# A convolving feed-forward rebuilt on products of 512 columns, with its first taps moved to ScalarE

## The chip, the cores and the metric

The kernel runs on one core of one Trainium2 chip. The metric is the device time of one execution in microseconds (us), the median of several runs. The core has TensorE (PE in the profile, with its weight loads shown as PEld), VectorE (DVE), ScalarE (ACT), GpSimd (POOL) and the DMA queues that SyncE (SP) feeds. TensorE's clock has two levels, 1.2 and 2.4 GHz; the profile shows the granted one as 0.50 and 1.00.

## The reference, cut to what matters

The program is a chain of two small transformer blocks on 256 positions with a width of 1024. The part that is touched is the feed-forward of the first block. Unlike the four later ones, it convolves gate and up over positions with three taps before the activation.

```python
def causal_dwconv(x, w):          # out[t] = sum_i w[i] x[t-2+i], per channel
    ...
def conv_ffn(hn, w_up, conv_w, conv_b, w_down):   # hn (1, 256, 1024), w_up (1024, 5632)
    u = causal_dwconv(hn @ w_up, conv_w) + conv_b
    gate, val = jnp.split(u, 2, axis=-1)          # 2816 channels each
    return (jax.nn.silu(gate) * val) @ w_down     # (2816, 1024)

h = h + conv_ffn(rms_norm(h, norm_ffn[l]), ffn_up[l], ffn_conv_w[l], ffn_conv_b[l], ffn_down[l])
```

## The kernel before

**Numbers in two parts.** Everything is stored with channels on partitions and positions along the free axis. A float32 product is made from operands split into a high and a low part: high weights by high operand, high weights by low operand, low weights by high operand. The weights come from memory as 260 slabs of 128 x 2048 (16 blocks of 128 x 128, 1 MB each) through a ring of three slots. For each slab SyncE issues one transfer into `ring_raw`, ScalarE copies it rounded into `ring_hi` (the "hi split"), and VectorE subtracts to get `ring_lo` (the "lo split"). ScalarE may write a slot when TensorE has multiplied the slab three before (`multiplied` counts slabs); SyncE may refill the raw slot when the lo split of the slab three before is done.

**The order of work** is written out by hand for each engine and no engine leaves its order: an instruction that waits holds up all that stands behind it on that engine.

**The feed-forward** goes over 11 pairs of 256 gate channels and 256 up channels. Its slabs are gate 0, up 0, then for each pair p from 1 to 10 the three slabs gate p, up p, down p-1, and at last down 10. Below, G, U and D with a number are these slabs and the products made from them. A loop of 5 turns carries two pairs each on every engine, so there are 10 passes for the pairs 1 to 10; pair 0 stands ahead of the loop and D10 behind it.

**The convolving feed-forward before** (`conv_feed_forward`, three functions, for PE at L518, ACT at L1339, DVE at L1946) makes G and U with `output_slab`: for each of the 16 blocks three products of 256 columns, into one bank of PSUM for a slab. Four banks (0 and 2 for gates, 1 and 7 for ups) alternate, banks 3 to 6 hold the sum of the down projection. VectorE takes the whole work between: it multiplies the sums by the row norm `inv` on the way out of PSUM (L1837), makes the first tap with the bias (L1965) and the two later taps (L1970, L1976), two instructions for each tap, multiplies with the activated gate, and subtracts for `hidden_lo` (L1834). ScalarE gives Silu and the copy `hidden_hi`.

**The plain feed-forward** (`feed_forward`, ffn_0 to ffn_3) makes G and U with `wide_slab`: high and low part of the operand lie side by side in X2, so a block needs one product of 512 columns (high weights) and one of 256 (low weights). Each slab then fills two banks, and each bank holds two halves that must be added. ScalarE copies one half out (`gate_copy`, `up_copy`), VectorE adds the other to it (`add_half`) and the banks are free when this is done (`halves_added`). Gate has banks 0 and 1, up has 2 and 3, down 4 to 7.

The wide product is this:

```python
out, w = bank(first + m), slice((m * KT + k) * P, (m * KT + k + 1) * P)
mm(out, ring_hi[:, slot, w], X2[:, k].rearrange("p s t -> p (s t)"), k == 0, False)
return mm(out[:, 0:T], ring_lo[:, slot, w], XH[:, k, :], False, k == KT - 1)
```

Of the kernel before, what the change touches and what calls it, by code (L numbers as in the profile page):

```python
# [108 lines left out]
def program(nc, ins, out_t):  # L109
    ctx = ExitStack()  # L110
    with ctx:
# [270 lines left out]
        def _(pe):  # L382
# [135 lines left out]
            def conv_feed_forward(name):  # L518

                g0, n = START[name], ffns[0]  # L520
                split, gate_scaled, up_taken = sem("hidden_lo"), sem("gate_scaled"), sem("up_taken")

                def down(at, odd, i, pairs):
                    slot, _, g = place(at, i, 6)
                    pe.wait_ge(lo_split, g + 1)
                    pe.wait_ge(split, pairs)
                    for k in range(2):
                        for m in range(KT):
                            last = block_product(bank(3 + m // 2)[:, m % 2 * T:(m % 2 + 1) * T], slot, k * KT + m,
                                                 HH[:, odd, k, :], HL[:, odd, k, :], False, False)  # L530
                    last.then_inc(multiplied, 1)

                output_slab(g0, 0, bank(0), fresh=EVERY)
                output_slab(g0 + 1, 0, bank(1), between=norm_sum)
                for b in range(3, 7):
                    for m in range(2):
                        mm(bank(b)[:, m * T:(m + 1) * T], zeros[:, 0:P], zeros[:], True, False)
# [12 lines left out]

                slot, _, g = place(g0 + 32)
                pe.wait_ge(lo_split, g + 1)
                pe.wait_ge(split, (n + 1) * FP)
                for m in range(KT):
                    for k in range(2):
                        last = block_product(bank(3 + m // 2)[:, m % 2 * T:(m % 2 + 1) * T], slot, k * KT + m,
                                             HH[:, 0, k, :], HL[:, 0, k, :], False, k == 1)
                    if m % 2 and m < KT - 1:
                        last.then_inc(sem("down_bank"), 1)
                last.then_inc(multiplied, 1)  # L560
                ffns[0] += 1

            def feed_forward(name):
# [710 lines left out]
        def _(act):  # L1274
# [546 lines left out]
        def _(dve):  # L1821
# [124 lines left out]
            def conv_feed_forward(name):  # L1946
# [3 lines left out]
                def gate(at, i, pair, b, split=None):  # L1950
# [4 lines left out]
                    if split is not None:  # L1955
                        split_slab(split, i, 6)
# [911 lines left out]
```

## Time and profile before

| | |
|---|---|
| median of 3 runs | 1770.28 us (1767.76 to 1773.57) |
| the profiled execution | 1767.87 us, its span 1765.9 us |
| PE busy | 1710.1 us, 97% of the span |
| DVE busy | 1235.5 us, 70% |
| ACT busy | 876.7 us, 50% |
| mean granted clock | 0.987 |
| the convolving feed-forward | from about 465 to 662 us |

A line of the timeline gives the start, the length, engine, line, operation and tiles; "x2" is two like instructions merged, whose length goes from the start of the first to the end of the second. "[0.39 <-ACT ring_hi L1280]" says that the engine stood idle for 0.39 us before the instruction, until ACT's instruction that writes `ring_hi` ended. Consecutive instructions of one engine overlap a little, so the distance from start to start is what a place in the order costs. L388, L1280, L1834 and L1837 are lines of helpers (one product, one activation, tensor_tensor, multiplication); the tiles say which use it is. `silu_out`, `hidden`, `conv_x` and `conv_acc` all lie in the tile "arena".

### The profile page before, as it was taken

What the parts mean: (1) busy time and instruction counts of PE and PEld (TensorE: products, weight loads), DVE (VectorE), ACT (ScalarE), POOL (GpSimd) and SP (SyncE); (2) the same over time, 40 slices, a digit from 0 to 9 for tenths busy, and PEclk for the clock granted to TensorE, in tenths of its full rate; (3) what the DMA queues carried; (4) which work ended last, traced back from release to release, by engine and by line L of the source; (5) the groups of instructions that cost most, each with busy time, mean ns of one, the idle gap of its engine ahead of it and who ended that gap; (6) DMA issues with size and microseconds to landing.
All of it is one profiled execution on the core that took longest, in us unless ns stands there. A gap on an engine that the chain in (4) does not pass through costs nothing.

```text
span 1765.9 us, 32905 instructions
## 1 busy us (share of the span) xinstructions
PE 1710.1 (97%) x13828; PEld 1599.1 (91%) x13828; DVE 1235.5 (70%) x1299; ACT 876.7 (50%) x924; POOL 37.7 (2%) x40
## 2 busy tenths in 40 slices
PE   7999998999999999999999999999999999999997
PEld 7988898998999998999999999997999987999997
DVE  5767657954788878666895766677666776666666
ACT  4376434533534345444674644466444652554455
POOL 0000000100000000000030000000000000000000
PEclk9999999999999999999999999999999998999999
DMA  7524444452344544554543455452555440354551
GB/s 275 189 96 144 151 145 174 164 194 97 144 181 152 214 154 157 189 190 166 188 150 110 176 210 180 180 187 103 190 197 183 167 165 24 121 196 168 192 187 48
DMA packets 42664, 286.94 MB, mean 162 GB/s; under 512 B 4720, under 2 KB 6896, under 8 KB 9168
## 3 DMA queue, kind: packets, MB, share of 16 engines
q1 hardware_dynamic: 38528, 273.70, 42.7%
q0 software_dynamic: 2816, 10.69, 1.7%
q8 instruction: 72, 1.18, 0.3%
q10 hardware_dynamic: 1232, 1.25, 0.2%
q14 instruction: 16, 0.13, 0.0%
HBM read 281.42 MB, written 4.19 MB: 162 GB/s over the span
## 4 chain that ended last, share of the span: by engine, by line
PE 81%; DVE 11%; ACT 5%; issue 3%; DMA 1%; POOL 0%; DVEq 0%; ACTq 0%
PE PS L388 80%; DVE arena L1837 3%; DVE ring_lo L1834 3%; ACT arena L1280 2%; ACT ring_hi L1280 2%; DVE arena L1834 1%; ACT L1280 1%; DVE operand L1897 1%; DVE inv L1891 0%; DVE residual L1834 0%; DMA ring_raw<-in_w_stream 0%; DMA arena<-in_ple_t 0%; DVE arena L1970 0%; DVE arena L1965 0%; DVE inv L2598 0%
## 5 line engine op out<-in xcount | busy, mean ns | idle before, releaser
L388 PE MATMUL PS<-operand,ring_hi 128*128 128x256 f32 (+1 forms) x4776 | 1126.4, 321 | 23.0 <-DVE operand L1897 14.2
L388 PEld LDWEIGHTS PS<-operand,ring_hi 128*128 128x128 f32 x4776 | 798.6, 193 | 94.4 <-DVE ring_lo L1834 13.4
L388 PE MATMUL PS<-operand,ring_lo 128*128 128x256 f32 x3092 | 876.2, 283 | 2.2 <-issue 2.2
L1834 DVE TENSOR_TENSOR ring_lo<-ring_raw,ring_hi 128x2048 fp32r<-128x2048 f32 x260 | 600.7, 2314 | 192.5 <-ACT ring_hi L1280 192.2
L1280 ACT ACTIVATE ring_hi<-ring_raw 128x2048 fp32r<-128x2048 f32 x260 | 494.6, 1907 | 206.4 <-PE PS L388 201.4
L388 PEld LDWEIGHTS PS<-operand,ring_lo 128*128 128x128 f32 x3092 | 593.8, 192 | 2.6 <-issue 2.5
L388 PE MATMUL PS<-hidden_hi,ring_hi 128*128 128x256 f32 x880 | 249.0, 283 | 1.3 <-DVE hidden_lo L1834 1.3
L388 PE MATMUL PS<-hidden_lo,ring_hi 128*128 128x256 f32 x880 | 249.0, 283 | 0.0
L388 PE MATMUL PS<-hidden_hi,ring_lo 128*128 128x256 f32 x880 | 248.9, 283 | 0.0
L1280 ACT ACTIVATE arena<-PS 128x512 f32<-128x512 f32 (+4 forms) x121 | 79.5, 666 | 302.0 <-PE PS L388 292.5
L388 PEld LDWEIGHTS PS<-hidden_hi,ring_hi 128*128 128x128 f32 x880 | 168.6, 192 | 3.5 <-issue 1.5
L388 PEld LDWEIGHTS PS<-hidden_hi,ring_lo 128*128 128x128 f32 x880 | 168.7, 192 | 0.0
L388 PEld LDWEIGHTS PS<-hidden_lo,ring_hi 128*128 128x128 f32 x880 | 168.6, 192 | 0.0
L1834 DVE TENSOR_TENSOR arena<-arena,PS 128x512 f32<-128x512 f32 (+4 forms) x120 | 81.0, 685 | 110.4 <-ACT arena L1280 108.6
L1280 ACT ACTIVATE arena<-arena 128x512 f32<-128x512 f32 (+5 forms) x117 | 83.2, 722 | 103.7 <-DVE arena L1976 56.8
L388 PE MATMUL PS<-arena 64*64 64x64 f32 (+7 forms) x2264 | 125.9, 249 | 8.8 <-DVE arena L1837 4.1
L388 PEld LDWEIGHTS PS<-arena 64*64 64x64 f32 (+4 forms) x2264 | 109.7, 151 | 24.0 <-issue 5.4
L1280 ACT ACTIVATE hidden_hi<-arena 128x512 fp32r<-128x512 f32 x55 | 34.8, 632 | 111.7 <-DVE arena L1837 111.7
L1837 DVE TENSOR_TENSOR arena<-PS,inv 128x512 f32<-128x512 f32 x74 | 50.5, 687 | 49.8 <-PE PS L388 49.4
L1837 DVE TENSOR_TENSOR arena<-arena 128x512 f32<-128x512 f32 (+3 forms) x96 | 72.8, 768 | 15.2 <-ACT arena L1280 9.1
L1837 DVE TENSOR_TENSOR arena<-arena,inv 128x512 f32<-128x512 f32 x96 | 66.1, 688 | 4.3 <-ACT arena L1280 2.8
L1280 ACT ACT_TABLE_LOAD x49 | 62.9, 1283 | 4.4 <-issue 3.5
(148 smaller groups left out, 942.6 us busy)
## 6 DMA issues: line engine op xcount, KB each, us to landing
ring_raw<-in_w_stream SPq DMA_DIRECT2D x260, 1024.0 KB, 4.8
spilled_gates<-arena POOLq DMA_DIRECT2D x12, 256.0 KB, 2.6
arena<-spilled_gates POOLq DMA_DIRECT2D x2, 1536.0 KB, 9.3
tables<-in_tables POOLq DMA_DIRECT2D x1, 1344.0 KB, 10.7
residual<-in_x_t ACTq DMA_DIRECT2D x4, 256.0 KB, 6.0
arena<-in_mem_t POOLq DMA_DIRECT2D x1, 1024.0 KB, 14.5
out_t<-residual SPq DMA_DIRECT2D x4, 256.0 KB, 2.1
arena<-in_spatial_t POOLq DMA_DIRECT2D x1, 512.0 KB, 4.2
```

The source lines that it names most:

```text
L388: return nc.tensor.matmul(out, lhs, rhs, start=start, stop=stop, skip_group_check=True)
L1280: return nc.scalar.activation(out, in_, func, **kw)
L1834: return v.tensor_tensor(out, a, b, op)
L1837: return v.tensor_tensor(out, a, b, ALU.mult)
L1897: v.scalar_tensor_tensor(out=XL[:, x0 + k, :], in0=src[:, k, :], scalar=col(gain[0], gain[1] + k), in1=XH[:, x0 + k, :].bitcast(F32), op0= ...
```

## The change

The convolving feed-forward gets the plain one's products. On TensorE its own function goes and `feed_forward("ffn_c")` stands in its place, with `wide_slab` and banks 0 and 1 for gate, 2 and 3 for up, 4 to 7 for down. ScalarE copies one half out of each pair of banks and also makes the first tap with the bias (`first_taps`, Identity with scale and bias from `params`). VectorE adds the other half, multiplies by `inv` in SBUF (`scale`) and makes the two later taps. The order on both engines is written anew. The sum for the norm behind the stage moves from bank 7 to bank 3. The counts of `halves_added` and `half_copied` in the plain feed-forwards shift, since ffn_c now counts too.

```diff
@@ TensorE @@
-            def conv_feed_forward(name):
...
-                with pe.Fori(0, FP // 2) as i:
-                    pe.wait_ge(gate_scaled, i * 2 + (n * FP + 1))
-                    output_slab(g0 + 2, 0, bank(2), i, 6)
-                    pe.wait_ge(sem("norm_root"), norms[0])
-                    pe.wait_ge(up_taken, i * 2 + (n * FP + 1))
-                    output_slab(g0 + 3, 0, bank(7), i, 6)
-                    down(g0 + 4, 0, i, i * 2 + (n * FP + 1))
-                    pe.wait_ge(gate_scaled, i * 2 + (n * FP + 2))
-                    output_slab(g0 + 5, 0, bank(0), i, 6)
-                    pe.wait_ge(up_taken, i * 2 + (n * FP + 2))
-                    output_slab(g0 + 6, 0, bank(1), i, 6)
-                    down(g0 + 7, 1, i, i * 2 + (n * FP + 2))
-
...
-                        at, halves = g0 + 5 - 3 * odd, i * 4 + (2 * (n - 1) * FP + 3 - 2 * odd)
+                        at, halves = g0 + 5 - 3 * odd, i * 4 + (2 * n * FP + 3 - 2 * odd)
...
-            conv_feed_forward("ffn_c")
+            feed_forward("ffn_c")
...
-                last = chunk_sums(7, 2 * c, c == 0, c == 3)
+                last = chunk_sums(3, 2 * c, c == 0, c == 3)
@@ ScalarE @@
 
-                def gate(pair, i=0, split=None):
-
-                    if split is not None:
-                        split_slab(split, i, 6)
+                def copy(at, i, half, x, first, free):
+
+                    act.wait_ge(multiplied, place(at, i, 6)[2] + 1)
+                    act.wait_ge(*free)
+                    run(x, sides(first)[:, 1]).then_inc(sem("half_copied"), 1)
+
+                def gate_copy(at, i, pair):
+                    copy(at, i, 0, conv_x[0], 0, (sem("conv_done"), pair))
+
+                def up_copy(at, i, pair):
+                    copy(at, i, 1, conv_x[1], 2, (up_taken, pair + 1))
+
+                def first_taps(acc, x, tile_, scaled, free):
+
+                    act.wait_ge(*scaled)
+                    act.wait_ge(*free)
+                    for m in range(2):
+                        run(acc[:, m, :], x[:, m, :], ACT.Identity,
+                            scale=prm[:, bass.ds(tile_ + (m + COL["ffn_conv_w"] + 2 * 4 * FP), 1)],
+                            bias=prm[:, bass.ds(tile_ + (m + COL["ffn_conv_b"]), 1)]).then_inc(sem("first_tap"), 1)
+
+                def gate_taps(pair, free=True):
+                    first_taps(conv_acc, conv_x[0], pair * 2, (sem("gate_scaled"), pair + 2),
+                               (sem("gate_active"), pair) if free else (sem("gate_scaled"), 1))
+
+                def up_taps(pair):
+                    first_taps(conv_acc2, conv_x[1], pair * 2 + 2 * FP, (sem("conv_up_scaled"), pair + 1),
+                               (up_taken, pair + 1))
+
+                def gate(pair):
+
...
                 split_slab(g0 + 2)
+                act.wait_ge(multiplied, g0 + 1)
+                run(conv_x[0], sides(0)[:, 1]).then_inc(sem("half_copied"), 1)
                 split_slab(g0 + 3)
                 norm_root()
+                up_copy(g0 + 1, 0, 0)
+                gate_taps(0, False)
+                up_taps(0)
                 gate(0)
                 up(0, 0)
                 with act.Fori(0, FP // 2) as i:
-                    split_slab(g0 + 4, i, 6)
-                    gate(i * 2 + 1, i, g0 + 5)
-                    up(i * 2 + 1, 1, i * 6 + (g0 + 2))
-                    split_slab(g0 + 6, i, 6)
-                    split_slab(g0 + 7, i, 6)
-                    gate(i * 2 + 2, i, g0 + 8)
-                    up(i * 2 + 2, 0, i * 6 + (g0 + 5))
-                    split_slab(g0 + 9, i, 6)
+                    for odd in (1, 0):
+                        pair = i * 2 + (2 - odd)
+                        split_slab(g0 + 7 - 3 * odd, i, 6)
+                        gate_copy(g0 + 5 - 3 * odd, i, pair)
+                        gate_taps(pair)
+                        split_slab(g0 + 8 - 3 * odd, i, 6)
+                        up_copy(g0 + 6 - 3 * odd, i, pair)
+                        gate(pair)
+                        up_taps(pair)
+                        split_slab(g0 + 9 - 3 * odd, i, 6)
+                        up(pair, odd, i * 6 + (g0 + 5 - 3 * odd))
...
-            norm_root()
+            norm_root(b=3)
@@ VectorE @@
-                def gate(at, i, pair, b, split=None):
-
-                    dve.wait_ge(multiplied, place(at, i, 6)[2] + 1)
-                    dve.wait_ge(up_taken, pair + 1)
-                    mul(conv_x[0], tiles_of(b, 2), over(inv[:, 0:T], 2)).then_inc(gate_scaled, 1)
-                    if split is not None:
-                        split_slab(split, i, 6)
-                    dve.wait_ge(gate_scaled, pair + 2)
-                    taps(conv_acc, conv_x[0], pair * 2, pair * 11, sem("conv_done"))
...
-                def taps(acc, x, tile_, before, done):
-
-                    for m in range(2):
-                        w2 = prm[:, bass.ds(tile_ + (m + COL["ffn_conv_w"] + 2 * 4 * FP), 1)]
-                        b = prm[:, bass.ds(tile_ + (m + COL["ffn_conv_b"]), 1)]
-                        v.tensor_scalar(acc[:, m, :], x[:, m, :], w2, b, ALU.mult, ALU.add)\
-                         .then_inc(sem("conv_tap"), 1)
-                    dve.wait_ge(sem("conv_tap"), before + 2)
-                    for m in range(2):
...
+                def add_half(x, first, pair, up):
+
+                    dve.wait_ge(sem("half_copied"), pair * 2 + (1 + up))
+                    tt_(x, x, sides(first)[:, 0], ALU.add).then_inc(sem("halves_added"), 1)
+
+                def scale(x, pair, up, done):
+
+                    dve.wait_ge(sem("halves_added"), pair * 2 + (1 + up))
+                    mul(x, x, over(inv[:, 0:T], 2)).then_inc(done, 1)
+
+                def later_taps(acc, x, tile_, first, before, done):
+
+                    dve.wait_ge(sem("first_tap"), first)
+                    for back in (1, 2):
+                        for m in range(2):
+                            w = prm[:, bass.ds(tile_ + (m + COL["ffn_conv_w"] + (2 - back) * 4 * FP), 1)]
+                            v.scalar_tensor_tensor(out=acc[:, m, back:T], in0=x[:, m, 0:T - back], scalar=w,
+                                                   in1=acc[:, m, back:T], op0=ALU.mult, op1=ALU.add)\
+                             .then_inc(done if (back, m) == (2, 1) else sem("conv_tap"), 1)
+                        if back == 1:
+                            dve.wait_ge(sem("conv_tap"), before + 2)
+
+                def gate_taps(pair):
+                    later_taps(conv_acc, conv_x[0], pair * 2, pair * 4 + 2, pair * 7, sem("conv_done"))
+
+                def up_taps(pair):
+                    later_taps(conv_acc2, conv_x[1], pair * 2 + 2 * FP, pair * 4 + 4, pair * 7 + 3, sem("conv_tap"))
+
+                def up(pair, odd):
+
+                    dve.wait_ge(sem("conv_tap"), pair * 7 + 7)
+                    dve.wait_ge(gate_active, pair + 1)
                     dve.wait_ge(sem("hidden_lo"), pair)
-                    mul(conv_x[1], tiles_of(b, 2), over(inv[:, 0:T], 2)).then_inc(sem("conv_up_scaled"), 1)
-                    dve.wait_ge(sem("conv_up_scaled"), pair + 1)
-                    taps(conv_acc2, conv_x[1], pair * 2 + 2 * FP, pair * 11 + 5, sem("conv_tap"))
-                    dve.wait_ge(sem("conv_tap"), pair * 11 + 11)
-                    dve.wait_ge(gate_active, pair + 1)
                     mul(hidden, silu_out, flat(conv_acc2)).then_inc(up_taken, 1)
                     dve.wait_ge(sem("hidden_hi"), pair + 1)
                     tt_(flat(HL[:, odd]), hidden, flat(HH[:, odd]).bitcast(F32), ALU.subtract)\
                         .then_inc(sem("hidden_lo"), 1)
 
...
                 with dve.Fori(0, FP // 2) as i:
-                    split_slab(g0 + 4, i, 6)
-                    gate(g0 + 2, i, i * 2 + 1, 2, g0 + 5)
-                    up(g0 + 3, i, i * 2 + 1, 1, 7)
-                    split_slab(g0 + 6, i, 6)
-                    split_slab(g0 + 7, i, 6)
-                    gate(g0 + 5, i, i * 2 + 2, 0, g0 + 8)
-                    up(g0 + 6, i, i * 2 + 2, 0, 1)
-                    split_slab(g0 + 9, i, 6)
+                    for odd in (1, 0):
+                        pair = i * 2 + (2 - odd)
+                        split_slab(g0 + 7 - 3 * odd, i, 6)
+                        add_half(conv_x[0], 0, pair, 0)
+                        scale(conv_x[0], pair, 0, gate_scaled)
+                        split_slab(g0 + 8 - 3 * odd, i, 6)
+                        gate_taps(pair)
+                        add_half(conv_x[1], 2, pair, 1)
+                        scale(conv_x[1], pair, 1, sem("conv_up_scaled"))
+                        split_slab(g0 + 9 - 3 * odd, i, 6)
+                        up_taps(pair)
+                        up(pair, odd)
...
-            down("ffn_c", None, scale=1.0, first=3)
+            down("ffn_c", None, scale=1.0)
```

## Rows read from the trace of the kernel before

**Rows 1.** The page: the chain that ended last, shares of the span by engine.

```profile
PE 81%; DVE 11%; ACT 5%; issue 3%; DMA 1%; POOL 0%; DVEq 0%; ACTq 0%
```

**Rows 2.** Windows: stretch, length, busy time (instructions) of each engine, clock, DMA; one pass each.

```profile
566.00:583.27 17.27, 17.27 (x147) 17.27 (x146) 14.26 (x20) 6.79 (x5) 0.00 (x0) 1.00 0.46 182
...
770.60:787.74 17.14, 17.14 (x115) 15.64 (x114) 10.97 (x10) 7.87 (x7) 0.00 (x0) 1.00 0.51 184
```

**Rows 3.** Timeline of VectorE: one pass of the convolving feed-forward.

```profile
570.57 4.50 DVE L1834 TENSOR_TENSOR ring_lo<-ring_raw,ring_hi 128x2048 fp32r<-128x2048 f32 x2 [1.12 <-ACT ring_hi L1280]
...
576.04 2.29 DVE L1834 TENSOR_TENSOR ring_lo<-ring_raw,ring_hi 128x2048 fp32r<-128x2048 f32 x1 [0.38 <-ACT ring_hi L1280]
578.25 0.73 DVE L1965 TENSOR_SCALAR arena<-arena,params 128x256 f32<-128x256 f32 x2
579.13 0.88 DVE L1970 SCALAR_TENSOR_TENSOR arena<-arena,params 128x255 f32<-128x255 f32 x2 [0.15 <-DVE arena L1965]
580.16 0.88 DVE L1976 SCALAR_TENSOR_TENSOR arena<-arena,params 128x254 f32<-128x254 f32 x2
580.95 0.68 DVE L1837 TENSOR_TENSOR arena<-PS,inv 128x512 f32<-128x512 f32 x1
...
583.74 0.88 DVE L1976 SCALAR_TENSOR_TENSOR arena<-arena,params 128x254 f32<-128x254 f32 x2
584.64 0.69 DVE L1837 TENSOR_TENSOR arena<-arena 128x512 f32<-128x512 f32 x1
586.04 0.69 DVE L1834 TENSOR_TENSOR hidden_lo<-arena,hidden_hi 128x512 fp32r<-128x512 f32 x1 [0.70 <-ACT hidden_hi L1280]
587.84 4.49 DVE L1834 TENSOR_TENSOR ring_lo<-ring_raw,ring_hi 128x2048 fp32r<-128x2048 f32 x2 [1.11 <-ACT ring_hi L1280]
```

**Rows 4.** Timeline of ScalarE in the same pass.

```profile
574.09 1.92 ACT L1280 ACTIVATE ring_hi<-ring_raw 128x2048 fp32r<-128x2048 f32 x1 [1.75 <-PE PS L388]
...
585.37 0.63 ACT L1280 ACTIVATE hidden_hi<-arena 128x512 fp32r<-128x512 f32 x1 [3.67 <-DVE arena L1837]
585.91 3.70 ACT L1280 ACTIVATE ring_hi<-ring_raw 128x2048 fp32r<-128x2048 f32 x2
```

**Rows 5.** Timeline of VectorE in the plain feed-forward that follows (ffn_0).

```profile
691.49 0.68 DVE L1834 TENSOR_TENSOR arena<-arena,PS 128x512 f32<-128x512 f32 x1
692.20 0.69 DVE L1837 TENSOR_TENSOR arena<-arena,inv 128x512 f32<-128x512 f32 x1
692.81 2.28 DVE L1834 TENSOR_TENSOR ring_lo<-ring_raw,ring_hi 128x2048 fp32r<-128x2048 f32 x1
```

**Rows 6.** Timeline of ScalarE behind the stage: two scaled copies, then a square.

```profile
668.68 0.91 ACT L1280 ACTIVATE operand<-residual,params 128x256 fp32r<-128x256 f32 x2 [2.74 <-DVE residual L2432]
669.49 0.61 ACT L1280 ACTIVATE arena<-residual 128x512 f32<-128x512 f32 x1
```

**Rows 7.** Timeline of VectorE ahead of the loop of the convolving feed-forward.

```profile
474.72 1.75 DVE L1891 RECIPROCAL inv<-root 128x256 f32<-128x256 f32 x1
...
483.03 0.69 DVE L1837 TENSOR_TENSOR arena<-arena 128x512 f32<-128x512 f32 x1
...
486.22 2.29 DVE L1834 TENSOR_TENSOR ring_lo<-ring_raw,ring_hi 128x2048 fp32r<-128x2048 f32 x1 [1.11 <-ACT ring_hi L1280]
```

**Rows 8.** Timeline of TensorE: first product of D10.

```profile
656.00 0.35 PE L388 MATMUL PS<-hidden_hi,ring_hi 128*128 128x256 f32 x1 [1.30 <-DVE hidden_lo L1834]
```

**Rows 9.** Windows: TensorE at the start of the program, and in a pause and after it.

```profile
11.10:16.60 5.50, 5.49 (x26) 5.50 (x27) 4.10 (x8) 4.49 (x7) 0.00 (x0) 1.00 1.00 424
16.60:22.00 5.40, 5.40 (x46) 5.40 (x46) 4.86 (x4) 2.79 (x2) 0.00 (x0) 1.00 1.02 424
501.00:503.20 2.20, 0.05 (x2) 0.02 (x1) 2.20 (x2) 2.20 (x2) 0.00 (x0) 1.00 0.00 0
...
504.80:508.20 3.40, 3.40 (x18) 3.40 (x17) 3.40 (x4) 0.00 (x0) 0.00 (x0) 0.50 0.95 386
```

**Rows 10.** The page: costliest groups, busy time and mean, idle time before; table loads.

```profile
L1280 ACT ACT_TABLE_LOAD x49 | 62.9, 1283 | 4.4 <-issue 3.5
```

More of the change, by code:

```diff
@@ L516, in _ @@
             ffns = [0]
-            def conv_feed_forward(name):
[L520 to L535, printed above, removed]
-                    for m in range(2):
-                        mm(bank(b)[:, m * T:(m + 1) * T], zeros[:, 0:P], zeros[:], True, False)
-                with pe.Fori(0, FP // 2) as i:
-                    pe.wait_ge(gate_scaled, i * 2 + (n * FP + 1))
-                    output_slab(g0 + 2, 0, bank(2), i, 6)
-                    pe.wait_ge(sem("norm_root"), norms[0])
-                    pe.wait_ge(up_taken, i * 2 + (n * FP + 1))
-                    output_slab(g0 + 3, 0, bank(7), i, 6)
-                    down(g0 + 4, 0, i, i * 2 + (n * FP + 1))
-                    pe.wait_ge(gate_scaled, i * 2 + (n * FP + 2))
-                    output_slab(g0 + 5, 0, bank(0), i, 6)
-                    pe.wait_ge(up_taken, i * 2 + (n * FP + 2))
-                    output_slab(g0 + 6, 0, bank(1), i, 6)
-                    down(g0 + 7, 1, i, i * 2 + (n * FP + 2))
[L551 to L561, printed above, removed]
@@ L1960, in taps @@
-                def taps(acc, x, tile_, before, done):
-                    for m in range(2):
-                        w2 = prm[:, bass.ds(tile_ + (m + COL["ffn_conv_w"] + 2 * 4 * FP), 1)]
-                        b = prm[:, bass.ds(tile_ + (m + COL["ffn_conv_b"]), 1)]
-                        v.tensor_scalar(acc[:, m, :], x[:, m, :], w2, b, ALU.mult, ALU.add)\
-                         .then_inc(sem("conv_tap"), 1)
-                    dve.wait_ge(sem("conv_tap"), before + 2)
-                    for m in range(2):
-                        w1 = prm[:, bass.ds(tile_ + (m + COL["ffn_conv_w"] + 4 * FP), 1)]
-                        v.scalar_tensor_tensor(out=acc[:, m, 1:T], in0=x[:, m, 0:T - 1], scalar=w1,
-                                               in1=acc[:, m, 1:T], op0=ALU.mult, op1=ALU.add)\
-                         .then_inc(sem("conv_tap"), 1)
-                    dve.wait_ge(sem("conv_tap"), before + 4)
-                    for m in range(2):
-                        w0 = prm[:, bass.ds(tile_ + (m + COL["ffn_conv_w"]), 1)]
-                        v.scalar_tensor_tensor(out=acc[:, m, 2:T], in0=x[:, m, 0:T - 2], scalar=w0,
-                                               in1=acc[:, m, 2:T], op0=ALU.mult, op1=ALU.add)\
-                         .then_inc(done if m == 1 else sem("conv_tap"), 1)
@@ L1994, in conv_feed_forward @@
                 split_slab(g0 + 2)
+                add_half(conv_x[0], 0, 0, 0)
                 split_slab(g0 + 3)
                 norm_factor()
-                gate(g0, 0, 0, 0)
-                up(g0 + 1, 0, 0, 0, 1)
-                with dve.Fori(0, FP // 2) as i:
-                    split_slab(g0 + 4, i, 6)
-                    gate(g0 + 2, i, i * 2 + 1, 2, g0 + 5)
-                    up(g0 + 3, i, i * 2 + 1, 1, 7)
-                    split_slab(g0 + 6, i, 6)
-                    split_slab(g0 + 7, i, 6)
-                    gate(g0 + 5, i, i * 2 + 2, 0, g0 + 8)
-                    up(g0 + 6, i, i * 2 + 2, 0, 1)
-                    split_slab(g0 + 9, i, 6)
+                add_half(conv_x[1], 2, 0, 1)
+                scale(conv_x[0], 0, 0, gate_scaled)
+                scale(conv_x[1], 0, 1, sem("conv_up_scaled"))
+                gate_taps(0)
+                up_taps(0)
+                dve.wait_ge(sem("conv_tap"), 7)
+                dve.wait_ge(gate_active, 1)
+                mul(hidden, silu_out, flat(conv_acc2)).then_inc(up_taken, 1)
+                dve.wait_ge(sem("hidden_hi"), 1)
+                tt_(flat(HL[:, 0]), hidden, flat(HH[:, 0]).bitcast(F32), ALU.subtract).then_inc(sem("hidden_lo"), 1)
+                with dve.Fori(0, FP // 2) as i:
+                    for odd in (1, 0):
[10 more added lines that the diff above has]
+                        up(pair, odd)
                 ffns[0] += 1
@@ L2015, in add_half @@
                 def add_half(out, first, pair, up):
-                    dve.wait_ge(sem("half_copied"), pair * 2 + (2 * (n - 1) * FP + 1 + up))
+                    dve.wait_ge(sem("half_copied"), pair * 2 + (2 * n * FP + 1 + up))
                     tt_(out, out, sides(first)[:, 0], ALU.add).then_inc(sem("halves_added"), 1)
                 def half_added(pair, up):
-                    dve.wait_ge(sem("halves_added"), pair * 2 + (2 * (n - 1) * FP + 1 + up))
+                    dve.wait_ge(sem("halves_added"), pair * 2 + (2 * n * FP + 1 + up))
                 def gate_scale(pair):
```

2 lines of the change are left out of this document (removed).

## The prediction

> **What bounds the kernel now.** I read the chain that ended last first: 81% of it is TensorE, VectorE has 11% [rows 1]. So on the whole a shorter piece of TensorE work counts. I then read one pass of the stage (one pair, three slabs) by windows. TensorE is busy through all of its 17.27 us, VectorE for 14.26, ScalarE for 6.79 [rows 2]. Busy shares don't say how much room VectorE has, since it waits inside its order; that is read from its timeline. It runs from 570.57 to 587.84, again 17.27, with two lasting waits for ScalarE: 1.11 before the lo split of D, and 0.38 before the one at 576.04 [rows 3]. The second comes from a hi split that ScalarE began late, as TensorE had not finished a slab [rows 4]: this is TensorE's pace showing through. Without it VectorE's order would take 17.27 - 0.38 = 16.89. The reader is to see two orders of nearly one length, TensorE's 17.27 and VectorE's 16.89: a few tenths more on VectorE and it becomes the bound.
>
> **TensorE after.** The plain feed-forward has the new products already, and its pass takes 17.14, with 115 products for 147 (a few records are missing, 144 are made) [rows 2]. Hence 0.13 less for a pair; over 11 pairs 1.4 us. That is all that the wide products can give: the columns stay the same, 768 for a block.
>
> **VectorE's order after, step by step.** I take distances from start to start in one pass, since these are what a place in the order costs; t = 0 is the start of the lo split of D(p-1).
>
> 1. Lo split of D: 578.25 - 576.04 = 2.21 [rows 3]. The add begins at 2.21.
> 2. Add of the gate halves: 692.20 - 691.49 = 0.71 [rows 5]. ScalarE's copy of one half, some 0.6 as the square of the same size (0.61 [rows 6]), lies under the lo split, once G(p) is made.
> 3. Scale of gate at 2.92. Here the new wait begins. ScalarE's order is gate copy, first taps of gate, hi split of G(p+1); VectorE's next instruction is the lo split of that same slab. The first taps wait for the scale, the hi split stands behind them, the lo split waits for the hi split. From an instruction of VectorE to ScalarE's on its result is 585.37 - 584.64 = 0.73 [rows 3, 4]; so the taps start at 3.65. No row of before shows Identity with scale and bias. The nearest are two scaled copies of like size: 0.91 busy for both, 0.81 from start to start of the next [rows 6]. In a loop with coefficients addressed by a register, two taps on VectorE cost 1.03 where they are busy 0.88 [rows 3]. So 0.81 from below and 1.04 from above; I take 0.90. From the start of the hi split to that of the lo split: 576.04 - 574.09 = 1.95 [rows 3, 4]. Step 3 costs 0.73 + 0.90 + 1.95 = 3.58, and the lo split begins at 6.50. Without the wait its distance would be 692.81 - 692.20 = 0.61 [rows 5]: the order loses 2.97.
> 4. Lo split of G(p+1): 2.21, to 8.71.
> 5. Later taps of gate: 580.16 - 579.13 = 1.03 and 580.95 - 580.16 = 0.79, together 1.82 [rows 3], to 10.53. Silu follows under the next steps.
> 6. Add of the up halves 0.71, to 11.24. The up copy lies under step 4.
> 7. Scale of up, and the same knot again: ScalarE has the up taps ahead of the hi split of U(p+1), for which VectorE waits. 3.58 once more, to 14.82.
> 8. Lo split of U(p+1): 2.21, to 17.03.
> 9. Later taps of up: 1.03 + 0.90 (584.64 - 583.74) = 1.93 [rows 3], to 18.96.
> 10. The product `hidden`, ScalarE's `hidden_hi`, `hidden_lo`, ScalarE's hi split of D(p), the lo split of D(p): as before, 587.84 - 584.64 = 3.20 [rows 3].
>
> Sum: 2.21 + 0.71 + 3.58 + 2.21 + 1.82 + 0.71 + 3.58 + 2.21 + 1.93 + 3.20 = **22.16 us** for a pass, against 17.27. VectorE's busy time hardly moves: two pairs of first taps go (2 x 0.73), two adds come (2 x 0.69). What it gains is two waits of 2.97, because ScalarE's short taps now stand between VectorE's scale and the split that VectorE needs next. ScalarE itself would be busy about 6.79 + 2 x 0.61 + 2 x 0.91 = 9.8 of 22.16, and TensorE 17.14: no engine would be full, the order is the bound.
>
> **Does TensorE or a transfer hold this chain?** G(p) can start when its lo split is done, at 6.50 + 2.29 = 8.79 of the pass before; (17.14 - 17.27/3)/2 = 5.7 later it is made, at 14.5, and is copied only after 22. U(p) waits for its lo split, 14.82 + 2.29 = 17.1, and ends at 22.8, 0.6 into the pass; its copy comes after 6.5. D(p-1) waits until 2.29 and ends at 8.05, ahead of G(p+1). So TensorE stands 0.7, 2.6 and 1.7 us in each pass, 5.0 in all, and VectorE never waits for it. The banks come free with the adds, before their products are due. The raw slots are refilled as soon as a lo split ends; each refill has more time than now, so the transfers stay hidden, and SyncE has nothing else in its queue.
>
> **Ahead of the loop.** The add of gate 0 goes between two lo splits. ScalarE's copy stands ahead of the hi split of U1, which puts the norm's reciprocal at about 475.2, now 474.72 [rows 7]. Then add, two scales, the taps of gate (0.73 + 0.90 behind their scale) and 1.8 each for the later taps of gate and up bring `hidden` to 482.9, now 483.03: the first taps run beside VectorE here, as no split stands behind them. I take the start of the loop at 486.2, as now [rows 7].
>
> **Behind the loop.** The tenth pass starts at 486.2 + 9 x 22.16 = 685.6. Its `hidden_lo` starts 18.96 + 1.40 (586.04 - 584.64) in and ends 0.69 later, at 706.7. D10 starts then, now at 656.00 [rows 8]: 50.7 later. D9 was done at 8.05 of that pass, 693.7, so TensorE stands 13 us. The nearest row is the start of the program, after 11.1 us without work: 26 products in the first 5.50 us and 46 in the 5.40 behind them [rows 9], though the clock column shows 1.00 there. The low level (1.2 GHz for 2.4) costs D10 then 5.5 x (1 - 26/46) = 2.4. Bounds: 0 (D10 itself began after a pause of 1.30 at full speed, [rows 8]) and 2.4. I take 2.4, as the pauses are alike. The work behind, with bank 3 for 7 and `first` as 4, is the same: 0.
>
> **Sum.** 50.7 + 2.4 = 53.1 more. The profiled execution had 1767.87, so 1821.0; the median of the runs stands 2.4 above that, so **1823 us**, 3.0% slower.
>
> **A page on Identity.** The Trainium skill, "ScalarE: Activation LUTs", section "Table sets: the hidden batching unit", says that identity and copy lie in every table set. No row of before shows Identity. By the page no table is loaded for the taps, and the sum stays; the rival with table loads below is what it denies.
>
> **The rivals.**
> - *TensorE stays the bound.* Then a pass takes 17.14, the stage gains 1.4, and if the pause of 2.2 at 501 with the slow stretch behind it (18 products in 3.4 us for 28, 1.2 us [rows 9]) and the 1.30 before D10 vanish too, 1.4 + 2.2 + 1.2 + 1.3 = 6.1. Time: 1764 to 1769. For it: ffn_0 does run at TensorE's pace with these products. Against: there only the copy stands ahead of the hi split on ScalarE, nothing that waits for the scale. It decides where VectorE's order falls below 17.14: it is 16.2 with both waits gone (22.16 - 2 x 2.97), so the two together would have to cost under 0.9, and one hi split alone is 1.95. Chance 0.05, of which 0.02 is over 0.3% faster.
> - *Only one of the two waits is paid*, the other being covered by something that I misread in the order. 22.16 - 2.97 = 19.19 for a pass, 29.7 us less: about 1793. Against: both places have the same three instructions. Chance 0.03.
> - *Table loads.* Silu and Identity by turns, each with a load of 1.28 us [rows 10]. The one ahead of Silu lies in idle time; the one ahead of the up taps would begin when Silu ends, at 11.2, and put the taps at 12.5 for 11.97, 0.5 a pass: 1828. Chance 0.05.
> - *The low clock lasts.* A pause of 2.2 us was followed by a stretch at 0.50 [rows 9], and each pass would have a pause of 2.6. One such stretch costs TensorE 1.2 us, two 2.4, and it has 5.0 to spare: no cost. If the low clock holds for whole passes, TensorE needs 17.14 x 46/26 = 30.3 and becomes the bound: 8.2 x 10 = 82 more, 1905. Against: the stretch was short and TensorE then ran on at 1.00. Chance 0.03. The Trainium skill, "TensorE: Matmul & The Clock Gate", section "HAM oscillation — how this bites in real kernels", tells of a kernel whose wait recurs with each tile and whose clock falls in every tile; by that rule one fall in each pass, which the spare time takes in.
>
> **How the numbers follow.** My forecast has 0.84. Its own range: 0.81 to 1.04 for a pair of first taps moves a pass by -0.18 to +0.28, ten passes by -2 to +3; D10's clock 0 to 2.4; a semaphore's 0.1 at some of the six handovers, up to +3; the run's place in its spread, 3 either way. Together 1815 to 1830. With the table loads and some room for sizes that I read wrongly the range is **1812 to 1833**. Outside it lie the first, second and fourth rival. A measurement of this kernel tells about 0.3% (5.3 us) from no change: faster 0.02, same 0.03, slower 0.95.
>
> **What would show it.** Right: VectorE's timeline with waits of about 2.9 before two of its three lo splits in each pass, released by ScalarE's `ring_hi`; passes of 22.2; TensorE pausing about 2.6 for `ring_lo` before U; about 13 us of pause before D10, and the stage's end some 53 us later. Each wide slab 5.7. 49 table loads as now [rows 10]. Wrong: passes near 17.14, or TensorE's products at a pace of 0.2 us throughout the stage; a hi split that starts before the first taps would break the knot at its root.

## The result, and the profile after

| | before | changed |
|---|---|---|
| median | 1770.03 us (4 runs, 1767.76 to 1773.57) | 1828.09 us (4 runs, 1826.41 to 1828.65) |
| ratio | | 1.033, 95% interval 1.0318 to 1.0343: slower |
| profiled execution, its span | 1767.87, 1765.9 us | 1828.55, 1826.6 us |
| mean granted clock | 0.987 | 0.978 |

Every run behind the numbers of this document is a fast one but the fourth of experiment 4, which took 4044.83 us for no reason that its record shows and is left out.

The chain that ended last, by engine, on the page of the changed kernel. Its columns are those of [rows 1].

```profile
PE 72%; DVE 13%; ACT 7%; issue 6%; DMA 1%; DVEq 0%; ACTq 0%; POOL 0%
```

TensorE has lost nine points against [rows 1]; VectorE and ScalarE have gained two each and "issue" three. One pass by windows, with the columns of [rows 2]:

```profile
601.03:623.84 22.81, 19.31 (x115) 16.87 (x113) 14.18 (x18) 9.82 (x12) 0.00 (x0) 0.93 0.40 138
```

The pass lasts 22.81 us for 17.27 [rows 2] and no engine is full in it: TensorE 19.31 (some of it at the low clock), VectorE 14.18, ScalarE 9.82. The reader is to see a longer pass with less work on VectorE. What fills it is seen in VectorE's timeline of that pass, the answer to [rows 3]:

```profile
601.03 2.29 DVE L1824 TENSOR_TENSOR ring_lo<-ring_raw,ring_hi 128x2048 fp32r<-128x2048 f32 x1 [1.11 <-ACT ring_hi L1235]
603.24 0.68 DVE L1824 TENSOR_TENSOR arena<-arena,PS 128x512 f32<-128x512 f32 x1
603.96 0.69 DVE L1827 TENSOR_TENSOR arena<-arena,inv 128x512 f32<-128x512 f32 x1
607.82 2.29 DVE L1824 TENSOR_TENSOR ring_lo<-ring_raw,ring_hi 128x2048 fp32r<-128x2048 f32 x1 [3.17 <-ACT ring_hi L1235]
610.03 1.89 DVE L1956 SCALAR_TENSOR_TENSOR arena<-arena,params 128x255 f32<-128x255 f32 x4
611.84 0.68 DVE L1824 TENSOR_TENSOR arena<-arena,PS 128x512 f32<-128x512 f32 x1
612.55 0.69 DVE L1827 TENSOR_TENSOR arena<-arena,inv 128x512 f32<-128x512 f32 x1
616.35 2.29 DVE L1824 TENSOR_TENSOR ring_lo<-ring_raw,ring_hi 128x2048 fp32r<-128x2048 f32 x1 [3.11 <-ACT ring_hi L1235]
618.56 1.90 DVE L1956 SCALAR_TENSOR_TENSOR arena<-arena,params 128x255 f32<-128x255 f32 x4
620.65 0.69 DVE L1827 TENSOR_TENSOR arena<-arena 128x512 f32<-128x512 f32 x1 [0.19 <-DVE arena L1956]
...
623.84 2.29 DVE L1824 TENSOR_TENSOR ring_lo<-ring_raw,ring_hi 128x2048 fp32r<-128x2048 f32 x1 [1.11 <-ACT ring_hi L1235]
```

Each scale (L1827 with `inv`) is followed by a lo split that waits over 3 us for ScalarE's `ring_hi`. ScalarE's timeline says what it did meanwhile:

```profile
604.89 1.10 ACT L1235 ACTIVATE arena<-arena,params 128x256 f32<-128x256 f32 x2 [3.41 <-DVE arena L1827]
605.89 1.89 ACT L1235 ACTIVATE ring_hi<-ring_raw 128x2048 fp32r<-128x2048 f32 x1
...
613.42 1.09 ACT L1235 ACTIVATE arena<-arena,params 128x256 f32<-128x256 f32 x2 [0.83 <-DVE arena L1827]
614.42 1.90 ACT L1235 ACTIVATE ring_hi<-ring_raw 128x2048 fp32r<-128x2048 f32 x1
```

At 604.89 it had stood for 3.41 us until VectorE's scale was done; then it made the taps, and only then the hi split that VectorE stood for. The waits from 475 to 715 us, nearly the whole stage (engine, tile, line, waited for: total, times, longest):

```profile
DVE ring_lo L1824 <- ACT ring_hi L1235: 75.0, 31, 3.2
...
PE PS L388 <- DVE ring_lo L1824: 35.5, 24, 2.6
...
PE PS L388 <- DVE hidden_lo L1824: 13.4, 1, 13.4
```

TensorE's 13.4 us is the pause before D10. The stage's last add starts at 722.20, 60.2 us later than in the profile of before (662.01).

### The profile page after: what moved, and what is told of

It is laid out like the page before. It is cut to its first block, busy times and chain, and to the rows that moved or that the text cites. A ratio compares the mean times of both kernels' runs of the same rounds, so it can differ in the third digit from the quotient of the medians.

```text
span 1826.6 us, 32297 instructions
## 1 busy us (share of the span) xinstructions
PE 1724.8 (94%) x13476; PEld 1589.9 (87%) x13476; DVE 1234.2 (68%) x1277; ACT 910.5 (50%) x990; POOL 37.6 (2%) x40
## 4 chain that ended last, share of the span: by engine, by line
PE 72%; DVE 13%; ACT 7%; issue 6%; DMA 1%; DVEq 0%; ACTq 0%; POOL 0%
PE PS L388 71%; ACT ring_hi L1235 4%; DVE arena L1827 4%; DVE ring_lo L1824 2%; ACT arena L1235 2%; DVE arena L1956 2%; DVE arena L1824 2%; DVE operand L1887 1%; ACT L1235 0%; DVE inv L1881 0%; DMA ring_raw<-in_w_stream 0%; DVE residual L1824 0%; DMA arena<-in_ple_t 0%; DVE inv L2595 0%; DVEq L1956 0%
## 5 line engine op out<-in xcount | busy, mean ns | idle before, releaser
L388 PEld LDWEIGHTS PS<-operand,ring_hi 128*128 128x128 f32 x4424 | 758.0, 193 | 143.7 <-DVE ring_lo L1824 46.0
L388 PE MATMUL PS<-hidden_hi,ring_hi 128*128 128x256 f32 x880 | 251.3, 286 | 19.4 <-DVE hidden_lo L1824 13.4
L1235 ACT ACTIVATE arena<-PS 128x512 f32<-128x512 f32 (+4 forms) x143 | 92.2, 652 | 306.5 <-PE PS L388 297.1
L1824 DVE TENSOR_TENSOR arena<-arena,PS 128x512 f32<-128x512 f32 (+2 forms) x142 | 96.0, 685 | 112.9 <-ACT arena L1235 109.5
L1827 DVE TENSOR_TENSOR arena<-arena,inv 128x512 f32<-128x512 f32 x118 | 81.2, 689 | 4.9 <-ACT arena L1235 2.8
L1827 DVE TENSOR_TENSOR arena<-arena 128x512 f32<-128x512 f32 (+3 forms) x96 | 72.8, 768 | 16.7 <-ACT arena L1235 9.1
L1235 ACT ACTIVATE arena<-arena,params 128x256 f32<-128x256 f32 x84 | 42.0, 549 | 59.6 <-DVE arena L1827 59.6
L1827 DVE TENSOR_TENSOR arena<-PS,inv 128x512 f32<-128x512 f32 x52 | 35.5, 688 | 50.4 <-PE PS L388 50.1
```

Source lines behind the costliest of these rows:

```text
L388: return nc.tensor.matmul(out, lhs, rhs, start=start, stop=stop, skip_group_check=True)
L1235: return nc.scalar.activation(out, in_, func, **kw)
L1824: return v.tensor_tensor(out, a, b, op)
L1827: return v.tensor_tensor(out, a, b, ALU.mult)
```

## The experiments

Each comparison with before is made on the same chip in alternation. The median of before was 1769.6 us in the first group (experiments 1 to 4), 1768.6 in the second (5 to 8) and 1769.2 in the third (9 and 10). Kernels of different groups are better compared by their ratios, or by the table of the stage alone at the end of this section.

**1. Both hi splits ahead of the taps.** Only ScalarE's order:

```diff
                         gate_copy(g0 + 5 - 3 * odd, i, pair)
-                        gate_taps(pair)
                         split_slab(g0 + 8 - 3 * odd, i, 6)
+                        gate_taps(pair)
                         up_copy(g0 + 6 - 3 * odd, i, pair)
+                        split_slab(g0 + 9 - 3 * odd, i, 6)
                         gate(pair)
                         up_taps(pair)
-                        split_slab(g0 + 9 - 3 * odd, i, 6)
```

> Edit: ScalarE's hi split of G(p+1) stands ahead of the first taps of gate, and its hi split of U(p+1) ahead of Silu and the first taps of up; nothing else. Theory (the order is the bound): in the changed kernel the two distances from scale to lo split are 3.86 and 3.80 us. With the hi splits ahead both fall to about 0.61, VectorE's order is 22.81 - 3.25 - 3.19 = 16.4 and TensorE's 17.14 becomes the bound: passes of 17.1 to 17.4, about 1771 us (1828.1 - 10 x 5.5 - 2 for the clock in D10), no low clock inside the stage. Rival (banks): gate and up have one pair of banks each where they had two banks in turn, and TensorE waits for the adds; then the passes stay above 20 and the time above 1800, whatever ScalarE's order.

Measured: 1767.9 us, ratio 0.9993 (0.9981 to 1.0006). VectorE's timeline in the first pass, the part with the two scales:

```profile
488.77 0.69 DVE L1827 TENSOR_TENSOR arena<-arena,inv 128x512 f32<-128x512 f32 x1
489.38 2.29 DVE L1824 TENSOR_TENSOR ring_lo<-ring_raw,ring_hi 128x2048 fp32r<-128x2048 f32 x1
...
494.11 0.69 DVE L1827 TENSOR_TENSOR arena<-arena,inv 128x512 f32<-128x512 f32 x1
494.72 2.29 DVE L1824 TENSOR_TENSOR ring_lo<-ring_raw,ring_hi 128x2048 fp32r<-128x2048 f32 x1
```

Both distances from scale to lo split are 0.61, for 3.86 and 3.80: the two waits are gone. The first six passes take 16.36 each on VectorE (`hidden_lo` to `hidden_lo`), which is the 16.4 expected for its order. TensorE works through all of them without a wait. Here are its first products of two D slabs in a row:

```profile
522.49 0.28 PE L388 MATMUL PS<-hidden_hi,ring_hi 128*128 128x256 f32 x1
539.56 0.28 PE L388 MATMUL PS<-hidden_hi,ring_hi 128*128 128x256 f32 x1
```

So TensorE needs 17.07 for a pass (in the kernel before 17.28, from 527.81 to 545.09). VectorE gains 0.7 on it in each pass: ScalarE's gate copy of the first pass finds its product ready (485.72), that of the eighth stands 1.43 us for TensorE (602.36). From the seventh pass on VectorE's timeline shows TensorE's pace:

```profile
603.90 0.69 DVE L1827 TENSOR_TENSOR arena<-arena,inv 128x512 f32<-128x512 f32 x1
604.80 2.29 DVE L1824 TENSOR_TENSOR ring_lo<-ring_raw,ring_hi 128x2048 fp32r<-128x2048 f32 x1 [0.21 <-ACT ring_hi L1235]
...
609.53 0.69 DVE L1827 TENSOR_TENSOR arena<-arena,inv 128x512 f32<-128x512 f32 x1
610.46 2.29 DVE L1824 TENSOR_TENSOR ring_lo<-ring_raw,ring_hi 128x2048 fp32r<-128x2048 f32 x1 [0.23 <-ACT ring_hi L1235]
```

The distances are 0.90 and 0.93 here, since ScalarE's copy, and the hi split behind it, wait for TensorE. This pass takes 16.98 from lo split to lo split, and its row of windows shows TensorE busy all the time:

```profile
600.97:617.95 16.98, 16.98 (x113) 15.50 (x112) 14.18 (x18) 9.83 (x11) 0.00 (x0) 1.00 0.51 185
```

VectorE's and ScalarE's busy times are those of the slow pass, 14.18 and 9.83; all of the 60 us lay in the order. The rival with the banks falls: banks and products were not touched. From the start of the loop to the end of D10 TensorE waits once, 3.2 us before D10.

**2 and 3. One hi split at a time.** The same edit for gate only, and for up only.

> Edit: only the hi split of G(p+1) is moved ahead of the first taps of gate. Theory: the gate wait alone goes, a pass is 22.81 - 3.25 = 19.56, ten passes 32.5 less, about 1796 us. Rival (banks): no change beyond 5 us, or all of the gain at once as the one bank that matters comes free, near 1771.

> Edit: only the hi split of U(p+1) is moved ahead of Silu and the first taps of up. Theory: the up wait alone goes, a pass is 22.81 - 3.19 = 19.62, about 1796 us, and the two single edits add up to the double one only as far as TensorE's 17.14 allows (32.5 + 31.9 = 64 against 55). Rival (banks): as for the gate alone.

Measured: gate alone 1795.95 us (ratio 1.0154, 1.0128 to 1.0179), up alone 1796.81 (1.0159, 1.0133 to 1.0186). From pair 0 to pair 10 a pass took 19.55 and 19.62. The waits are separate, of one size, and add up until TensorE is the bound.

**4 and 5. The first taps back on VectorE**, wide products kept; ScalarE's calls of the taps go. In the fifth ScalarE's hi split of U(p+1) also stands ahead of Silu:

```diff
+                    for m in range(2):
+                        v.tensor_scalar(acc[:, m, :], x[:, m, :], ...)\
+                         .then_inc(sem("first_tap"), 1)
                     dve.wait_ge(sem("first_tap"), first)
...
                         up_copy(g0 + 6 - 3 * odd, i, pair)
+                        split_slab(g0 + 9 - 3 * odd, i, 6)      # the fifth only
                         gate(pair)
-                        split_slab(g0 + 9 - 3 * odd, i, 6)      # the fifth only
```

> Edit: wide products kept, the first taps back on VectorE ahead of the later ones, ScalarE without them (its order is copy, hi split, copy, Silu, hi split, hidden_hi). Theory: the waits for ScalarE go, but each pair of first taps costs VectorE's order 0.88: 16.4 + 2 x 0.88 = 18.1 a pass, still longer than the 17.27 of before, which has the same work less two adds; about 1828 - 47 = 1781 us, some 9 above before. Rival (banks or the wide products themselves): passes above 20 here too, since nothing of them is changed.

Measured: 1794.88 us (three runs, 1794.51 to 1795.46; ratio 1.0144, 1.0112 to 1.0175), 14 above what I expected, and neither theory's number. The timeline of VectorE shows a wait that my sum had left out:

```profile
613.67 0.69 DVE L1823 TENSOR_TENSOR arena<-arena,inv 128x512 f32<-128x512 f32 x1
615.54 2.29 DVE L1820 TENSOR_TENSOR ring_lo<-ring_raw,ring_hi 128x2048 fp32r<-128x2048 f32 x1 [1.18 <-ACT ring_hi L1235]
```

Silu waits for the gate's last tap and stands ahead of the hi split of U(p+1): the same knot with another instruction. I had cleared the way of the taps alone.

> Edit: the kernel with the first taps back on VectorE, and ScalarE's hi split of U(p+1) moved ahead of Silu. Theory: its passes of 19.3 held one more wait that I had overlooked, 1.18 us before the lo split of U(p+1), because Silu, which waits for the gate's taps, stood ahead of that hi split. Without it a pass is 18.05 and the time 1795.2 - 12.7 = about 1782 us. Rival: the wide products or their banks keep something that the order doesn't explain; then it stays near 1795.

Measured: 1781.38 us (ratio 1.0078, 1.0062 to 1.0093), passes of 18.03. So with the waits gone the first taps on VectorE make its order longer than before's, as it has two adds more and the same taps. Beside experiment 1 this prices the move of the taps to ScalarE by itself: some 15 us gained, if nothing waits behind them (ratios 1.0078 and 0.9993; 15.9 by the stage alone).

**6. The clock held up to D10.** The changed kernel with products that nobody reads; this is extra work:

```diff
+                if n == 0:
+                    pe.wait_ge(sem("halves_added"), 2 * FP - 1)
+                    spare_products(0, 55)
                 slot, _, g = place(g0 + 32)
```

> Edit: the changed kernel, with 55 products that nobody reads (into bank 0, once the last gate halves are added) in TensorE's order ahead of D10, in place of most of its pause of 13.4 us. They are extra work. Theory: the pause itself is VectorE's and stays, but D10 then runs at the full clock, its last add comes 6.2 us after the end of hidden_lo as before, for 8.2 now: about 2.1 us less, 1826. Rival: the slower D10 is not the clock but something else, for example the bank wait; then still 8.2 and 1828.

Windows of D10, first in the changed kernel, then with the extra products:

```profile
714.00:719.40 5.40, 5.29 (x27) 5.32 (x28) 0.77 (x2) 1.67 (x2) 0.00 (x0) 0.56 0.03 14
```

```profile
714.90:720.70 5.80, 5.73 (x48) 5.76 (x49) 2.08 (x3) 2.69 (x4) 0.00 (x0) 1.00 0.03 13
```

From the start of the last `hidden_lo` to the last add: 8.93 us (713.27 to 722.20) without, 6.86 (714.13 to 720.99) with, 6.85 before. So the low level cost D10 2.07 us. The whole time does not show it: 1830.29 us (1828.83 to 1832.1), 2.2 more and not 2.1 less, and the intervals of the two ratios, 1.0339 to 1.0371 and 1.0318 to 1.0343, overlap. The profiles say where it went. Where the stage ends this profile is 1.2 us ahead of that of the changed kernel, and 3.5 behind at the program's end. Of these 4.7 us, 1.0 is lost between 1021 and 1030, in work that is the same in both, as the low clock lasts longer there:

```profile
1023.00:1029.60 6.60, 5.70 (x26) 5.70 (x27) 0.86 (x2) 0.12 (x1) 0.00 (x0) 0.50 0.00 1
```

In the changed kernel the like one has 3.2 us at 0.50. The next 2.3 us are no matter of the clock. ScalarE waits longer for a transfer, first in the changed kernel, then here:

```profile
1047.79 0.63 ACT L1235 ACTIVATE operand<-arena 128x512 fp32r<-128x512 f32 x1 [3.77 <-DMA arena<-in_ple_t]
```

```profile
1049.80 0.63 ACT L1238 ACTIVATE operand<-arena 128x512 fp32r<-128x512 f32 x1 [6.04 <-DMA arena<-in_ple_t]
```

The other profiles all have 3.6 to 4.0 us for this wait. The last 1.5 us go at 1057 to 1078, where this profile has a low stretch again (granted clock 0.57 from 1057 to 1061) and the changed kernel has none (1.00). Why the low stretches moved is not settled, and the late transfer stands in this one profile.

**7 and 8. Each pair of first taps made twice**, the second into memory that nobody reads (extra work), once in the changed kernel and once with both hi splits ahead.

> Edit: the changed kernel, with each pair of first taps made a second time into memory that nobody reads, behind the real pair and so ahead of the hi split. It adds work. Theory: each extra pair moves the hi split by its own 0.9 to 1.0 us, twice a pass: passes of 24.7 and some 1847 us. Rival (VectorE or TensorE is the bound by its work): no change, 1828.

> Edit: the same extra taps in the kernel with both hi splits ahead. Theory: ScalarE has 2.1 us of waiting behind the gate taps and 3.6 behind the up taps in each pass, the extra pairs of 1.0 fit, TensorE stays the bound: 1768, within 0.3% of it. Rival: taps on ScalarE cost time by being there, whatever the order: some 20 us more, 1788.

Measured: 1850.6 us (ratio 1.0468, 1.0452 to 1.0484) in the changed kernel, 1768.77 (1.0001, 0.999 to 1.0011) with the hi splits ahead. VectorE's row in the first, and four of ScalarE's in the second:

```profile
621.04 2.29 DVE L1828 TENSOR_TENSOR ring_lo<-ring_raw,ring_hi 128x2048 fp32r<-128x2048 f32 x1 [4.16 <-ACT ring_hi L1235]
```

```profile
608.18 2.08 ACT L1235 ACTIVATE arena<-arena,params 128x256 f32<-128x256 f32 x4
611.37 0.60 ACT L1235 ACTIVATE arena<-PS 128x512 f32<-128x512 f32 x1 [1.11 <-PE PS L388]
...
614.18 2.07 ACT L1235 ACTIVATE arena<-arena,params 128x256 f32<-128x256 f32 x4
618.82 0.63 ACT L1235 ACTIVATE hidden_hi<-arena 128x512 fp32r<-128x512 f32 x1 [2.57 <-DVE arena L1831]
```

The wait grew by 0.99 and the pass to 24.78, by 1.97 or twice a pair's 0.98. In the other order four taps leave 1.11 us of idle time behind them at the first place and 2.57 at the second. The first six passes take 16.36, as in experiment 1. So in the loop the same instructions cost 19.7 us or nothing, by their place alone. Ahead of the loop, where both kernels have one order, they cost 1.4 us in both: from the last add ahead of the stage to the first `hidden_lo` it is 21.7 for 20.25.

**9 and 10. A version that beats both.** On top of experiment 1 the last two passes are written out, and in the tenth the split of the next stage's slab goes behind `hidden` on both engines:

```diff
+                    if not last:
                         split_slab(g0 + 9 - 3 * odd, i, 6)
                     up_taps(pair)
                     up(pair, odd)
+                    if last:
+                        split_slab(g0 + 9 - 3 * odd, i, 6)
...
+                with dve.Fori(0, FP // 2 - 1) as i:
+                    turn(i, 1)
+                    turn(i, 0)
+                turn(FP // 2 - 1, 1)
+                turn(FP // 2 - 1, 0, True)
```

> Edit: on top of both hi splits ahead, the loop has 4 turns and the two last passes are written out; in the tenth the split of the following stage's slab goes behind hidden on VectorE and on ScalarE. Theory: only D10's pause of 3.2 us is left in the stage; in the tenth pass the up taps follow their scale at once and hidden_lo ends some 1.2 us earlier, the pause is then 2.0: 1766.5 us, which a comparison against before can hardly tell from 1 (0.9985). Rival: the pause is TensorE's own, then nothing moves.

> Edit: the same, and 8 products that nobody reads in TensorE's order ahead of D10, to fill the pause. Theory: they take 1.7 us of the pause of 2.0, the clock stays at 1.00 in D10 and its last add comes 6.9 us after the start of hidden_lo, for 8.35 with both hi splits ahead: 1.5 us less than the version without them, 1765. Rival: as the 55 products in the slow kernel, the stage gains 1.5 us and stretches of low clock elsewhere take it back.

Measured: 1762.37 us, ratio 0.9961 (0.9947 to 0.9974), and 1762.21, 0.9962 (0.9948 to 0.9975). The first is 0.4% faster than before and, by the ratios, 3.6% faster than the changed kernel. TensorE's one wait in its stage:

```profile
PE PS L388 <- DVE hidden_lo L1833: 1.6, 1, 1.6
```

D10's pause is 1.6 us for 3.2 and the last add comes 6.87 us after the start of the last `hidden_lo`, for 8.35 in experiment 1: the shorter pause left the clock up. So the 8 extra products had nothing left to hold; the two kernels are the same within their intervals. I had expected 1.5 us of them and nothing of this kind from the shorter pause. The stage is 3.1 us shorter than in experiment 1: 1.5 by D10's clock, 1.6 by an earlier last `hidden_lo`. The ratios (0.9961 and 0.9993) differ by some 5.7 us, each with some 2.3 either way, so 3.1 is not outside them.

**The stage alone.** The time from the start of the last add to the residual ahead of the stage (464.71 in the kernel before) to the start of the stage's own last add (662.01), in the one profiled execution of each kernel:

| kernel | us | against before |
|---|---|---|
| before | 197.30 | |
| changed | 257.31 | +60.0 |
| 1, both hi splits ahead | 194.84 | -2.5 |
| 2, gate only | 225.18 | +27.9 |
| 3, up only | 225.73 | +28.4 |
| 4, first taps on VectorE | 223.09 | +25.8 |
| 5, the same, Silu cleared | 210.69 | +13.4 |
| 6, clock held before D10 | 255.29 | +58.0 |
| 7, changed, taps twice | 277.94 | +80.6 |
| 8, both ahead, taps twice | 196.21 | -1.1 |
| 9, last pass mended | 191.73 | -5.6 |
| 10, the same, 8 products | 191.74 | -5.6 |

## Why the prediction was right

The time lay inside the range and the mechanism was the one forecast: VectorE's order with two knots in it, no engine full. By its steps:

- **TensorE's 17.14 for a pass** held nearly where it is the bound: 17.07 from D to D in experiment 1, as in ffn_0 (17.06 from D to D, where one stretch of [rows 2] had 17.14). So the wide products give 0.21 for a pair and not 0.13. In the changed kernel this was never needed.
- **The two waits** were forecast as 2.97 beyond the plain distance of 0.61 and came as 3.25 and 3.19. The cause is shown from both sides: moving the hi splits takes away one wait each (experiments 1 to 3), doubling the taps adds their price (7), and not where the hi split is ahead (8).
- **The pass, 22.16 forecast and 22.81 measured**, is the term that was mis-sized. Of the 0.65, step 3 had 0.28: the handover from the scale to the taps took 0.93 (603.96 to 604.89) for my 0.73, the pair of taps 1.00 for 0.90, the lo split began 1.93 after the hi split for 1.95. Step 7 had 0.22 and step 9 0.16 (618.56 to 620.65 is 2.09 for 1.93). Over ten passes this is 6.5 us. The pair of taps lay inside my bounds of 0.81 and 1.04; I took a value from copies that take one number from `params`, where the taps take two. The longer handover was outside my row, though the range had 0.1 at some of six handovers, an allowance that no row gave. (The terms of that range add up to 1832 at its upper end, not to 1830.) The Trainium skill, "ScalarE: Activation LUTs", section "What ACT_TABLE_LOAD costs", says that each operand given by a pointer adds about 93 ns to an activation. Added twice to the 0.81 of the copies this is an estimate of 1.00 for the pair, and the trace agrees with its 1.00.
- **Where the longer steps come from** is seen in experiment 9, whose tenth pass is written out and lies in no loop:

```profile
645.68 0.69 DVE L1836 TENSOR_TENSOR arena<-arena,inv 128x512 f32<-128x512 f32 x1
646.41 1.09 ACT L1235 ACTIVATE arena<-arena,params 128x256 f32<-128x256 f32 x2 [0.69 <-DVE arena L1836]
647.54 1.79 DVE L1965 SCALAR_TENSOR_TENSOR arena<-arena,params 128x255 f32<-128x255 f32 x4 [1.16 <-ACT arena L1235]
649.36 0.69 DVE L1836 TENSOR_TENSOR arena<-arena 128x512 f32<-128x512 f32 x1
```

  The up taps start 0.73 behind their scale, for 0.87 in the loop, and the later taps of up take 1.82 (in the ninth pass, written out too, 631.86 to 633.68), for 2.09. The pair of taps keeps its length (1.09 busy). So these 0.14 and 0.27 belong to the loop. Whether they go with operands addressed by a register or with the counts waited for, which are also computed there, is not shown.
- **Ahead of the loop** I had 486.2 for the first lo split and it came at 486.94: the up copy had to wait for U0 and began at 477.07, so the taps started at 479.10 and not at 478.3.
- **D10** ended 2.07 us later for the clock, for 2.4 forecast; its pause was 13.4 for 13. That it is the clock is shown inside the stage (experiment 6). After pauses of 10.1, 10.2 and 8.6 us in experiments 2, 3 and 5 D10 took 2.5, 2.5 and 2.4 longer than its 6.85. The 6.5 of the passes and the 0.7 ahead of the loop, less the 0.3 that D10 fell short of 2.4, are 6.9 of the 7.1 us by which the stage's last add came later than forecast (60.2 for 53.1).
- **Table loads**: 49, as before [rows 10]. The trace agrees with the Trainium skill, "ScalarE: Activation LUTs", section "Table sets: the hidden batching unit", that identity lies in every table set, and that rival falls.
- **The low clock** came in six of the ten passes, each time for one stretch of 3.4 us, and was taken in by TensorE's spare time: with or without such a stretch a pass is 22.81. The Trainium skill, "TensorE: Matmul & The Clock Gate", section "HAM oscillation — how this bites in real kernels", has the clock fall in every tile of its kernel; here, with pauses of 2.6 us at most, it fell in six of ten passes and cost nothing but in D10.
- **The rival "TensorE stays the bound"** described the kernel of experiment 1, and its point of decision was right: the two waits together had to fall under 0.9, and there both are gone. Its time was 1764 to 1769; measured were 1767.9, and 1762.4 with the last pass mended.

What the change can give is small: 0.2 us a pass of TensorE time (17.28 to 17.07), and 7 us in all with the pauses (experiment 9), 5.6 of them in the stage; the taps on ScalarE are needed for it (experiment 5 without them: 1781). The 58 us came from the place of the hi split in ScalarE's order, twice in each pass.

## What to carry to other kernels

Where two engines run orders written by hand, moving an instruction costs what stands behind it there: before moving work to an idle engine, list what that engine issues next and who waits for it. An instruction that waits for engine A must not stand ahead of one that A needs next; put the work that depends on nothing (here the hi split) first and the dependent one into the idle time behind it. A busy share of 50% says nothing against such a knot: in the slow and the mended kernel both engines' busy times in a pass were the same.

## What the runs showed of the hardware that I had not expected

- An Identity with scale and bias from `params` on 128x256 costs 1.00 us for two from start to start, where the two scaled copies have 0.81 [rows 6].
- Inside the loop it started 0.93 and 0.87 us after VectorE's scale, where the copy `hidden_hi` has 0.73 [rows 3, 4]; in a pass written out, the up taps too had 0.73 (experiment 9), and ahead of the loop the taps of the changed kernel started 0.72 after the scale of gate (478.38 to 479.10).
- The clock: a pause of 1.6 us before D10 left it at 1.00 (6.87 us to the last add), pauses of 3.2 and 13.4 cost D10 about 1.5 and 2.1 us. Yet in the changed kernel pauses of up to 2.6 us were followed by a low stretch in only six of ten passes.
- The untouched work behind the stage, from its last add to the program's end, took 1103.9 to 1104.8 us in nine of the twelve profiles, and 1106.0, 1107.1 and 1109.1 in three (experiments 8, 9 and 6). In the last of these 2.4 us were low clock and 2.3 a late transfer. Such a spread is more than the last pass or D10's clock is worth. Marks at a fixed instruction before and behind the stage told these apart where the total could not.
